# ScalarE's next weights ahead of the last two gate evictions of a column, in a hybrid decoder block

## Time and profile before

| | before |
|---|---|
| median of 3 runs | 3105.7 us |
| the profiled execution | 3113.7 us |
| its span | 3111.9 us |
| PE busy | 2840.0 us, 91% |
| DVE busy | 2122.1 us, 68% |
| POOL busy | 1756.4 us, 56% |
| ACT busy | 1109.1 us, 36% |
| the block of the 128 slots | about 809 to 1990 us |
| its 48 spread slots | about 1340 to 1865 us |

### The profile page before, as it was taken

One profiled execution on the slowest core, in us unless ns is written; L12 is line 12 of the kernel. 1 busy time (PEld: TensorE's weight loads), 2 busy tenths in 40 slices (PEclk: granted clock), 3 DMA queues, 4 the chain that ended last, 5 costly groups with the idle time before them and its releaser, 6 DMA issues. The chain is left out here.

```text
span 3111.9 us, 47231 instructions
## 1 busy us (share of the span) xinstructions
PE 2840.0 (91%) x15880; PEld 1549.7 (50%) x15880; DVE 2122.1 (68%) x3995; ACT 1109.1 (36%) x1480; POOL 1756.4 (56%) x1614
## 2 busy tenths in 40 slices
PE   6998788899999999988999999589999998999998
PEld 3444763455555555555666665334444443444443
DVE  2498974311667777767787874367778776877877
ACT  4332344122344444445666663212212221221212
POOL 1312553011244344455666667588888887888884
PEclk8999887999999999999999999899999999999999
DMA  3200002011233333357778777889999998999995
GB/s 114 77 24 21 0 30 113 28 40 40 80 112 113 108 116 106 118 200 262 281 274 296 269 285 272 268 314 359 338 365 352 342 366 289 341 350 364 331 353 225
DMA packets 260396, 648.60 MB, mean 208 GB/s; under 512 B 16992, under 2 KB 115552, under 8 KB 257136
## 3 DMA queue, kind: packets, MB, share of 16 engines
q1 hardware_dynamic: 186176, 378.33, 34.2%
q0 software_dynamic: 74160, 269.52, 23.5%
HBM read 542.39 MB, written 105.91 MB: 208 GB/s over the span
## 5 line engine op out<-in xcount | busy, mean ns | idle before, releaser
L91 POOL TENSOR_TENSOR w_low<-w_ring,w_high 128x1024 f16<-128x1024 f32 x164 | 385.6, 2352 | 976.6 <-ACT w_ring L86 976.5
L1247 PE MATMUL psum<-region_y,w_high 128*128 128x384 f16 x2048 | 675.5, 330 | 20.6 <-POOL w_low L91 19.0
L1667 PE MATMUL psum<-vh,wh 128*128 128x512 bf16 x1536 | 585.3, 381 | 100.0 <-POOL wl L1716 64.1
L1248 PE MATMUL psum<-region_y,w_high 128*128 128x384 f16 x2048 | 674.8, 329 | 0.0
L1249 PE MATMUL psum<-region_y,w_low 128*128 128x384 f16 x2048 | 674.3, 329 | 0.0
L1668 PE MATMUL psum<-vl,wh 128*128 128x512 bf16 x1536 | 585.1, 381 | 0.0
L1669 PE MATMUL psum<-vh,wl 128*128 128x512 bf16 x1536 | 584.4, 380 | 0.0
L1683 ACT ACTIVATE vh<-w_ring 128x1024 bf16<-128x1024 f32 x128 | 135.1, 1055 | 823.2 <-DMA w_ring<-in_v_t_dram 778.3
L1811 DVE TENSOR_TENSOR region_x<-region_x,psum 128x1024 f32<-128x1024 f32 x192 | 233.9, 1218 | 148.6 <-PE psum L1669 148.2
L1711 POOL TENSOR_TENSOR vl<-w_ring,vh 128x1024 bf16<-128x1024 f32 x128 | 273.3, 2136 | 49.5 <-ACT vh L1683 47.5
L1667 PEld LDWEIGHTS psum<-vh,wh 128*128 128x128 bf16 x1536 | 150.8, 98 | 298.6 <-issue 63.3
(11 more groups left out here) (236 smaller groups left out, 4882.4 us busy)
## 6 DMA issues: line engine op xcount, KB each, us to landing
w_ring<-in_u_t_dram SPq DMA_DIRECT2D x128, 512.0 KB, 4.1
w_ring<-in_v_t_dram SPq DMA_DIRECT2D x128, 512.0 KB, 6.6
acts_dram<-ge SPq DMA_DIRECT2D x128, 384.0 KB, 2.5
gates_dram<-scores SPq DMA_DIRECT2D x24, 2048.0 KB, 8.9
gt<-gates_dram SPq DMA_DIRECT2D x32, 1536.0 KB, 13.6
at<-acts_dram SPq DMA_DIRECT2D x32, 1536.0 KB, 21.1
w_ring<-in_w_stream_dram SPq DMA_DIRECT2D x20, 512.0 KB, 3.2
w_ring<-in_w_q_dram SPq DMA_DIRECT2D x16, 512.0 KB, 3.2
```

The lines of the kernel that those rows point to most:

```text
L91: pool.tensor_tensor(self.wl[:, s, :], self.wf[:, s, :], self.wh[:, s, :], ALU.subtract).then_inc(self.w_lo, 1)
L1247: pe.matmul(a, uh[:, par, row], xh[:, n, cols], start=(n == 0), stop=False)
L1248: pe.matmul(a, uh[:, par, row], xl[:, n, cols], start=False, stop=False)
L1667: pe.matmul(a, wh[:, par, c, rows], vh[:, par, c, cols], start=(c == 0), stop=False)
```

## The change

In a spread slot ACT calls `ring.high` after the Gelu of the second half, ahead of the wait for that half's octet and ahead of its two evictions. Before, it called it after them. The number of instructions stays the same on every engine; no buffer, DMA or other engine's order is changed.

```diff
@@ spread(s, par, n, j) of ScalarE
                 half = half_spread(n, j)
                 for h in range(2):
                     gelu(s, par, h, half)
+                    if h == 1:
+                        ring.high(act, par, half + 1)
                     o = 2 * j + h
                     u, r = o // 4, o % 2
                     act.wait_ge(g_mm, 8 * n + (o + 1))
                     if o % 4 == 0:
                         after(act, g_st[u], 16 * n)
                     for b in range(2):
                         ...
                         act.activation(... ACT.Copy).then_inc(g_ok, 1)
-                ring.high(act, par, half + 1)
```

## The result

The changed kernel takes 3126.8 us (median of 4 runs, 3123.85 to 3138.08); the kernel before took 3104.8 in the same comparison. The ratio is 1.0077, with a 95% interval from 1.0049 to 1.0105: slower by 0.5 to 1.1%, some 24 us. The profiled execution took 3138.1 us against 3113.7.

What follows compares the result with a forecast made beforehand. PE, stalled by late gathered rows in the spread slots, was taken as the bound. Terms of 17 + 5 + 2 + 1 = 25 us, taken as 20 for overlap, on 3105.7 gave 3126 us; range 3076 to 3168, the forecast's own 3110 to 3145.

Steps and rivals of the forecast that it cites:

- What bounds the kernel: In the 48 spread slots PE sets the pace and waits ten times for DVE's one-hot matrices, 41.6 us.
- The bound of 65 us: The most any change in the spread slots can bring: their 527 us less 462 us for 48 undisturbed slots.
- The limit of 2.6 us: A row gathered more than about 2.6 us ahead of the gate store lands before it; below, with the store's end.
- The moves themselves: On ACT in odd slots `high` starts 2.29 us earlier; evictions, gate store and the load behind it 1.37 us later.
- The late store and load: Colliding rows land 1.37 us later with the gate store's end, lengthening ten stalls of PE: 17 us lost.
- Contention of POOL and DVE: In odd slots `low` moves onto DVE's matrix operations, which have over 5 us of slack: 0, bounds -3 and +3.
- Sharing of the DMA engines: Even slots' earlier gather runs beside gate store and load, delaying the load up to 2.4 us; two more collisions, 5 us.
- Early `high` in odd slots: `low` and the next, even slot's gather on POOL start 2.29 us earlier, valued at 0.
- moving `high` up cannot help: In all 24 even slots `high` becomes bound by its load, which comes 1.37 us later.
- ACT's queue: Evictions and Gelu stand behind a `high` waiting for its load; harmful past +5.6 us: 2 us, bounds 0 and 31.
- Signs: `high` waits over 40 us; PE's matrix waits total 50 to 65 us, longest above 7; spread stretch near 547 us.
- faster, by a larger margin: Rival: the odd slots' gather comes up to 2 us earlier, the store later, collisions end: 3053 to 3080 us, chance 0.25.

Runs made afterwards that it cites:

- e4: The kernel before, with POOL issuing each gather one slot earlier: 3048.8 us, ratio 0.98.
- e5: e2 with POOL's `low` in odd slots also waiting for that slot's evictions: 3108.0 us, ratio 1.0009 to the kernel before.
- e9: e2 with the even slot's gather on POOL held until that slot's first octet is evicted: 3096.5 us, ratio 0.9974 to the kernel before.
- e10: The changed kernel, with POOL's `low` in odd slots waiting for that slot's evictions: 3098.7 us, ratio 0.998 to the kernel before.
- e2: The kernel before, with `high` ahead of the evictions in odd slots alone: 3126.8 us, ratio 1.0055.
- e8: The changed kernel, with SP issuing the even slot's weight load in the odd slot before, ahead of the gate store: 3052.9 us, ratio 0.9843 to the kernel before.
- e1: The kernel before, with `high` ahead of the evictions in even slots alone: 3100.0 us, ratio 0.9972.
- e6: The changed kernel, with POOL issuing each gather one slot earlier: 3093.9 us, ratio 0.9959 to the kernel before.

## Why the forecast came out, and what in it was wrong

The forecast was 3126 us, the measured time 3126.8. The direction is right. That the size is right to 1 us is luck: several terms behind it are wrong, and they made up for one another.

- **What bounds the kernel** was right: between the octets PE loses only by one-hot matrices behind late rows, and all nine such waits follow one of the ten rows that took over 10 us. The bound of 65 us is too high, since its stretch of 527 us begins ahead of the first octet and ends behind the last; the octets give 506.5 less 452.6, 53.9 us. e4 takes back 53.2 of them.
- **The limit of 2.6 us** for the margin is no fixed one. It holds for the kernel before with one exception (1.57 us ahead, landed in 6.6). In the changed kernel six rows were issued 2.0 to 2.5 us ahead; five landed in 5.9 to 6.9 us and one in 9.0, and all five below 2.0 took over 9.
- **The moves themselves** were right to 0.02 us in an undisturbed odd slot: `high` 2.28 us earlier, evictions, store and load 1.35 to 1.37 later.
- **The late store and load, 17 of 25 us**, is the largest term that failed. e5, e9 and e10 keep the store late and lose nothing. Late rows were to stall PE longer, "the longest above 7"; the waits behind them fell from 36.9 to 22.3 us, and the longest is 4.8.
- **Contention of POOL and DVE, 0** within -3 and +3, failed too. The "over 5 us of slack" was not there in even slots: `low` on the matrix operations gave six waits, 14.0 us.
- **Sharing of the DMA engines, 5 us.** Its form, a gather that runs beside the store and the load in place of behind them, is as I wrote it: rows that gain 2.3 us at the issue and nothing at the landing, and loads that take 1.1 us longer (I had put up to 2.4). More collisions, which the 5 us were to pay for, did not come: six rows over 9 us in place of ten. Its size stays open. e9 shows that the early gather has a part in e2's loss, and e8 that it has none once the load is ahead of the store.
- **Early `high` in odd slots, valued at 0**, is what the cost hangs on. e2 has it alone and loses 17 us; e5 holds back what follows from it on POOL and loses 1 to 3.
- **Even slots, "moving `high` up cannot help"**: it helps by 9 us where the load is not delayed (e1).
- **ACT's queue, 2 us** within 0 to 31: the change shows 10.0 us of waits for evictions, and e6, where rows do not matter, shows 31 us in the spread slots. I had the point from which it decides (+5.6) and did not follow the delay on into the next store and load, where it feeds itself.
- **Signs**: over 40 us of waits of `high` (132.5) held; 50 to 65 us of PE's waits for the matrices did not (41.2), nor did a stretch of 547 us (10.9 us longer than before, not 20).

The rival "faster, by a larger margin" did not happen, but it was a real one: its mechanism is e8. It named the condition rightly, `high` of even slots not later than before by more than 1.5 us. In the change it is 2.2 us later on the mean (+6.13 against +3.95).

## What to carry to other kernels

An instruction moved ahead brings a gain only if what it waits for is there; otherwise it turns a harmless wait into one that holds up all that stands behind it on its engine, so look first at the wait that the moved step will meet, and at which queue its data stands in. A transfer that is issued earlier need not land earlier: here one issued 2.3 us sooner, beside a larger one, gained nothing, so compare landings, not issues. A total of waits that stays the same can hide that one kind shrank and another came; split it by slot before calling a cause. And a change that loses by itself may be one half of a pair that wins: here one DMA moved ahead of another turned +0.8% into -1.6%.

## What was not expected of the hardware

The same order of instructions makes the kernel slower, faster or neither by its neighbours alone: +24 us by itself, some +45 with early gathers, -56 with the load ahead of the store, -2 with both. A 512 KB gather took 7.4 us to land on the mean in even slots of the kernel before, 9.6 in the changed one and 7.6 in e8, where it is issued as early and still meets the store, but the load no longer stands behind it. A bfloat16 matrix operation of 0.68 us took 2.6 to 3.0 us when `low` (2.1 us) ran beside it. And the clock of PE fell with its long waits. Around the end of the wait of 5.35 us in the earlier trace rows, 1496.3 to 1503.1 us, the granted clock is 0.50, the lower of its two levels (columns as in the earlier trace rows):

```profile
1496.30:1503.10 6.80, 5.73 (x29) 3.60 (x30) 6.66 (x13) 1.97 (x2) 4.76 (x5) 0.50 0.37 93
```

The mean over the spread slots is 0.95 before, 0.97 after with its shorter waits, and 1.00 in e8. e6 has 1.00 as well, although PE waits 21 times there, none longer than 2.0 us.
